# Routing without its weights first: the head of a routed expert stage reordered on three engines

## The chip, the cores and the metric

The kernel runs on one core of one Trainium2 chip. The metric is the device time of one execution in microseconds (us), the median of several runs. The engines are called as in the profile: PE is TensorE, DVE VectorE, ACT ScalarE, POOL GpSimd, and SP SyncE, from which most transfers are issued.

## What is computed

Two transformer blocks run one after the other on 512 tokens of width 1024. All matrix products are in float32, each made of three products of a split into an upper and a lower part. The last stage of the second block, the one that the change touches, is a mixture of experts with a two-level router:

```python
p_grp = softmax(t @ w_rg + b_rg)                 # 4 groups
g_val, g_idx = top_k(p_grp, 1)
le = (t @ w_re + b_re).reshape(n, 4, 4)          # 4 experts in each group
p_exp = softmax(take(le, g_idx))
e_val, e_idx = top_k(p_exp, 2)
weight = g_val * e_val / sum(e_val)
act = silu(t @ w_e_gate[e]) * (t @ w_e_up[e])    # for the chosen experts e
out = sum over the chosen e of weight * act @ w_e_down[e]
```

## The kernel before

Each engine has its own instruction stream, written out by hand, and semaphores order them. Weights stream from HBM in blocks of 1 MB through a ring of four slots (`raw`). ACT rounds a block to its upper part `wh`, DVE subtracts to get the lower part `wl` (`lows`, line 1964, two halves a block), PE multiplies, and its progress (`acc_ready`) frees the slot for SP's next load. In the expert stage a load is issued for each half of a block.

The head of the expert stage goes as follows, in the order of the data.

1. PE brings the router's 20 logits per token into `acc`. DVE's `route()` (lines 2656 to 2717) works on tiny tiles, 128 partitions by 4 to 80 numbers. Each instruction waits for the one before it (`link`). It scales and biases the logits, takes a softmax over the groups (ACT makes the exponential), finds the first maximum (`best`), selects that group's four expert logits, takes a softmax again, finds the two best, and writes `chosen` (a 0/1 mask of token by expert) and `tokx` (token numbers). Then it splits the lower half of the stage's third block (`lows(B0["moe"] + 2)`) and works out the weights (`wtwo`, `gateg`).
2. In the meantime PE transposes the normalised tokens (line 1204), ACT copies them out (`HN`, line 1826, after each of the two exponentials, line 1820) and SP stores them to HBM as `XD`.
3. PE counts with `chosen` (line 1212) which slot each token gets. DVE turns the counts into `posn`, sets the flag `crowded`, and compares positions with a count to make one-hot matrices `G1` (line 2724, four of them, one for each expert of the first group; line 2735 for a whole group). PE multiplies them with the token numbers (`slot_rows`, line 1091), DVE writes the row numbers `rows_in`, and POOL gathers the rows of `XD` into `XSL` by indirect DMA (line 454).
4. PE transposes the gathered rows (`turn_slots`, line 1105), ACT and DVE make `XH` and `XL` of them (`slots_upper` line 1748, `slots_lower` line 2764; the semaphores `f_xh` and `f_xl`), and `gathered(0, first=True)` begins: eight blocks of gate and up products, `b` = 0 to 7, two per expert, then four blocks of down products. Its body is the `Else` arm of a branch on `crowded` that every engine takes; the inputs here take that arm.

In the first group PE goes on so: block 0, the transpositions of the third expert's rows (0, 2), block 1, those of (0, 3), block 2, then rows of the next group. A transposition waits until `f_xl` says that the XL parts of the expert before are written, since it reuses their PSUM banks. On DVE the order is: product of block 0's activation (line 2777), `lows` of block 3, `slots_lower(0, 2)`, and so on. `give_rows_first` writes the row numbers for the results. They are not used before the first scatter. `keep_busy` (line 486) issues products whose results nobody reads; each appears as two rows of a matmul.

Of the kernel before, what the change touches and what calls it, by code (L numbers as in the profile page):

```python
# [12 lines left out]
P = 128  # L13
# [89 lines left out]
def build(nc, xT, memT, wstream, params, consts, lora, poolw, normf, out):  # L103
    with ExitStack() as ctx:
# [233 lines left out]
        def bank(hh, x):  # L338

            return (mb if hh else acc)[:, x if hh else 2 + x, :]  # L340

        def rows_bank(g, e=1):
# [132 lines left out]
        def _(pe):  # L475
# [622 lines left out]
            def turn_slots(i, e):  # L1098

                pe.wait_ge(s[f"in_row{e}"], i * 16 + 16)  # L1100
                pair = 0 if isinstance(i, int) and (i, e) == (0, 1) else 2
                if not isinstance(i, int) or (i, e) > (0, 1):
                    pe.wait_ge(s["f_xl"], i * 8 + 2 * e)
                for k in range(KT):
                    last = nc.tensor.transpose(acc[:, pair + k // 4, (k % 4) * P:(k % 4 + 1) * P],
                                               XSL[:, e, k * P:(k + 1) * P], ident)
                last.then_inc(s["f_tx"], 1)
# [9 lines left out]
            def gathered(i, first=False, last_group=False):  # L1117

                n0, t0 = B0["moe"], T0["moe"]
                if first:  # L1120
                    pe.wait_ge(s["f_toke"], 8)
                    keep_busy(mb[:, 3, :], 6)

                    pe.wait_ge(s["f_xl"], 4)

# [93 lines left out]
            crowded = pe.value_load(flag[0:1, 0:1])  # L1219
            slot_rows(1)  # L1220
            turn_slots(0, 0)
            turn_slots(0, 1)
            with pe.If(crowded > 0):
                pe.wait_ge(s["f_mask"], 2)
                norm_spread(7)
                with pe.Fori(0, 3) as i:
                    group("moe", i, 8, need=(xn_ready, 33), spread=spread_gate)
                group("moe", 3, 8, spread=spread_gate)
                pe.wait_ge(x_ready, 32 + KT)
                for q in range(8):  # L1230
                    if q >= 2:
                        pe.wait_ge(s["xf_ready"], q - 1)
                    turn_rows(q)
            with pe.Else():
                gathered(0, first=True)
                with pe.Fori(1, 3) as i:
                    gathered(i)
                gathered(3, last_group=True)
# [3 lines left out]
        def _(act):  # L1242
# [500 lines left out]
            def slots_upper(i, e):  # L1743

                act.wait_ge(s["f_tx"], i * 4 + (e + 1))
                pair = 0 if isinstance(i, int) and (i, e) == (0, 1) else 2
                for h in range(2):
                    actv(XH[:, 4 * h:4 * h + 4, e * P:(e + 1) * P], acc[:, pair + h, :].rearrange("p (k c) -> p k c", k=4),
                         ACT.Copy).then_inc(s["f_xh"], 1)
# [117 lines left out]
        def _(dve):  # L1867
# [788 lines left out]
            def route():  # L2656
# [6 lines left out]

                def best(p, eq, top, hot):

                    link(v.tensor_reduce(red(top), r(p), AX.X, ALU.max))
                    link(v.tensor_tensor(r(eq), r(p), wide(top), ALU.is_equal))
                    link(v.tensor_tensor(r(eq), r(eq), rank, ALU.mult))
                    link(v.tensor_reduce(red(23), r(eq), AX.X, ALU.max))
                    link(v.tensor_tensor(r(hot), r(eq), wide(23), ALU.is_equal))  # L2670

                def softmax_in(src, to):
                    link(v.tensor_reduce(red(0), src, AX.X, ALU.max))
                    v.tensor_tensor(r(to), src, wide(0), ALU.subtract).then_inc(s["rt_sub"], 1)

                def softmax_out(p):
                    link(v.tensor_reduce(red(0), r(p), AX.X, ALU.add))
                    link(v.reciprocal(red(22), red(0)))
                    link(v.tensor_tensor(r(p), r(p), wide(22), ALU.mult))

# [32 lines left out]
                link(v.tensor_tensor(r(6), r(6), wide(20), ALU.mult))  # L2713
                link(v.tensor_tensor(wtwo[:, 0, :], red(14), red(20), ALU.mult))
                link(v.tensor_tensor(wtwo[:, 1, :], red(17), red(20), ALU.mult))
                for g in range(4):
                    link(v.tensor_tensor(gateg[:, g], r(6), r(5)[:, :, g:g + 1].to_broadcast([P, TT, 4]), ALU.mult))

# [40 lines left out]
            def slots_lower(i, e):  # L2759
                pair = 0 if isinstance(i, int) and (i, e) == (0, 1) else 2  # L2760
                for h in range(2):
                    dve.wait_ge(s["f_xh"], i * 8 + (2 * e + h + 1))
                    dst = slice(4 * h, 4 * h + 4), slice(e * P, (e + 1) * P)
                    v.tensor_tensor(XL[:, dst[0], dst[1]], acc[:, pair + h, :].rearrange("p (k c) -> p k c", k=4),
                                    XH[:, dst[0], dst[1]].bitcast(F32), ALU.subtract).then_inc(s["f_xl"], 1)
# [250 lines left out]
```

## Time and profile before

| | us |
|---|---|
| median of 3 runs | 1656.53 |
| lowest and highest | 1651.3 and 1659.92 |
| the profiled execution | 1651.62 |
| its span, first to last instruction | 1649.7 |
| PE busy in the span | 1528.5 (93%) |
| DVE busy | 1095.7 (66%) |
| ACT busy | 705.2 (43%) |

The profiled execution is 1.92 us longer than its span, which is what lies around it. The stretch that the change rewrites lasts from 1402 to about 1440 us of that span. Of PE's matmuls the ends are modelled, and two that follow each other overlap in the rows.

### The profile page before, as it was taken

What the parts mean: (1) busy time and instruction counts of PE and PEld (TensorE: products, weight loads), DVE (VectorE), ACT (ScalarE), POOL (GpSimd) and SP (SyncE); (2) the same over time, 40 slices, a digit from 0 to 9 for tenths busy, and PEclk for the clock granted to TensorE, in tenths of its full rate; (3) what the DMA queues carried; (4) which work ended last, traced back from release to release, by engine and by line L of the source; (5) the groups of instructions that cost most, each with busy time, mean ns of one, the idle gap of its engine ahead of it and who ended that gap; (6) DMA issues with size and microseconds to landing.
All of it is one profiled execution on the core that took longest, in us unless ns stands there. A gap on an engine that the chain in (4) does not pass through costs nothing.

```text
span 1649.7 us, 26802 instructions
## 1 busy us (share of the span) xinstructions
PE 1528.5 (93%) x11012; PEld 1283.9 (78%) x11012; DVE 1095.7 (66%) x1661; ACT 705.2 (43%) x1057; POOL 62.4 (4%) x53
## 2 busy tenths in 40 slices
PE   5999988998999999999999999999999889889892
PEld 4889776876878888888878787877799657788892
DVE  5831667686489647737689998354765436677875
ACT  5422334444354333333454232334344345367783
POOL 0000000000000000000000000000000000222221
PEclk9999999999999999999999999999999999999996
DMA  6220000002422222222312222232234202478895
GB/s 250 102 90 13 2 2 3 3 3 78 153 77 79 101 102 102 90 90 102 128 51 103 100 79 102 77 126 92 102 128 154 77 18 85 164 244 309 313 315 188
DMA packets 37831, 181.37 MB, mean 110 GB/s; under 512 B 6342, under 2 KB 6470, under 8 KB 24400
## 3 DMA queue, kind: packets, MB, share of 16 engines
q1 hardware_dynamic: 30672, 167.08, 28.6%
q0 software_dynamic: 4864, 8.40, 1.5%
q10 hardware_dynamic: 2176, 4.19, 0.7%
q8 instruction: 87, 1.43, 0.4%
q14 instruction: 32, 0.26, 0.0%
HBM read 175.46 MB, written 12.58 MB: 114 GB/s over the span
## 4 chain that ended last, share of the span: by engine, by line
PE 71%; DVE 18%; ACT 4%; DMA 4%; issue 3%; POOL 0%; DVEq 0%; POOLq 0%; SPq 0%; ACTq 0%
PE acc L480 18%; PE acc L482 18%; PE acc L481 18%; DMA raw<-wstream 3%; DVE CA L2445 2%; PE acc L731 2%; PE mb L731 1%; DVE wl L1976 1%; DVE wl L1964 1%; PE acc L1038 1%; PE mb L562 1%; ACT wh L1273 1%; ACT wh L1260 1%; PE mb L480 1%; PE mb L481 1%
## 5 line engine op out<-in xcount | busy, mean ns | idle before, releaser
L480 PE MATMUL acc<-XH,wh 128*128 128x512 f32 x1008 | 396.2, 393 | 2.3 <-DVE wl L1976 1.3
L482 PE MATMUL acc<-XH,wl 128*128 128x512 f32 x1008 | 392.3, 389 | 0.0
L481 PE MATMUL acc<-XL,wh 128*128 128x512 f32 x1008 | 392.2, 389 | 0.0
L1273 ACT ACTIVATE wh<-raw 128x2048 fp32r<-128x2048 f32 x99 | 189.4, 1915 | 241.6 <-DMA raw<-wstream 241.6
L1976 DVE TENSOR_TENSOR wl<-raw,wh 128x2048 fp32r<-128x2048 f32 x99 | 226.1, 2287 | 67.2 <-ACT wh L1273 64.0
L480 PEld LDWEIGHTS acc<-XH,wh 128*128 128x128 f32 x1008 | 189.3, 188 | 44.6 <-issue 3.3
L481 PEld LDWEIGHTS acc<-XL,wh 128*128 128x128 f32 x1008 | 189.3, 188 | 40.6 <-issue 1.9
L482 PEld LDWEIGHTS acc<-XH,wl 128*128 128x128 f32 x1008 | 189.2, 188 | 39.6
L1294 ACT ACTIVATE ev<-acc 128x512 f32<-128x512 f32 x146 | 85.6, 598 | 218.7 <-PE acc L482 189.6
L1964 DVE TENSOR_TENSOR wl<-raw,wh 128x1024 fp32r<-128x1024 f32 x96 | 116.3, 1221 | 31.7 <-ACT wh L1260 23.7
L1260 ACT ACTIVATE wh<-raw 128x1024 fp32r<-128x1024 f32 x96 | 101.0, 1061 | 20.8 <-DMA raw<-wstream 19.0
L480 PE MATMUL acc<-wh,XH 128*128 128x256 f32 x320 | 94.2, 294 | 3.2 <-DVE tmp L2777 2.6
L482 PE MATMUL acc<-wh,XL 128*128 128x256 f32 x320 | 90.4, 283 | 0.0
L481 PE MATMUL acc<-wl,XH 128*128 128x256 f32 x320 | 90.4, 282 | 0.0
L2445 DVE SCALAR_TENSOR_TENSOR CA<-APAD,par,CA 128x512 f32<-128x512 f32 x120 | 82.1, 746 | 0.5
L480 PE MATMUL acc<-HH,wh 128*128 128x512 f32 x176 | 68.5, 389 | 0.0
L481 PE MATMUL acc<-HL,wh 128*128 128x512 f32 x176 | 68.5, 389 | 0.0
L482 PE MATMUL acc<-HH,wl 128*128 128x512 f32 x176 | 68.5, 389 | 0.0
L480 PEld LDWEIGHTS acc<-wh,XH 128*128 128x128 f32 x320 | 61.1, 191 | 4.0 <-DVE wl L1964 1.8
L481 PEld LDWEIGHTS acc<-wl,XH 128*128 128x128 f32 x320 | 61.2, 191 | 0.0
L482 PEld LDWEIGHTS acc<-wh,XL 128*128 128x128 f32 x320 | 61.1, 191 | 0.0
L444 POOL MEMSET XSL<- 128x4096 f32 x1 | 3.5, 3512 | 1397.6 <-PE mb L482 1397.6
(534 smaller groups left out, 2796.8 us busy)
## 6 DMA issues: line engine op xcount, KB each, us to landing
raw<-wstream SPq DMA_DIRECT2D x99, 1024.0 KB
raw<-wstream SPq DMA_DIRECT2D x96, 512.0 KB
YG<-YT ACTq DMA_DIRECT2D x8, 512.0 KB
XT<-xT SPq DMA_DIRECT2D x2, 1024.0 KB, 9.6
XT<-xT SPq DMA_DIRECT2D x1, 2048.0 KB, 7.7
XD<-HN SPq DMA_DIRECT2D x4, 512.0 KB, 2.6
out<-XTK SPq DMA_DIRECT2D x4, 512.0 KB, 2.6
cst<-consts SPq DMA_DIRECT2D x1, 1230.0 KB, 18.4
```

Of the source, the lines that this page charges most:

```text
L480: mm(out_, a[0], b[0], start=start, stop=False)
L481: mm(out_, a[0], b[1], start=False, stop=False)
L482: return mm(out_, a[1], b[0], start=False, stop=stop)
L562: mm(mb[:, 0, :], ones, sq[:, k % 2, :], start=(k == 0), stop=(k == KT - 1)).then_inc(sq_used, 1)
L731: last = mm(out_[hp(c), t * HD:(t + 1) * HD], left(hp(c), t), right(hp(c), t), start=True, stop=True)
L1038: last = mm(acc[:, v, :], VX[:, j, h * 256 + v * P:h * 256 + (v + 1) * P], PTx[:, j, :], start=(j == 0), stop=(j == 1))
L1260: actv(wh[:, slot, 4 * h:4 * h + 4].rearrange("p a b c -> p (a b c)"), raw[:, slot, h * BLK // 2:(h + 1) * BLK // 2], ACT.Copy).then_inc(h ...
L1273: actv(wh[:, n % RING].rearrange("p a b c -> p (a b c)"), raw[:, n % RING, :], ACT.Copy).then_inc(hi_done, 1)
L1294: actv(ev[:, ring, 2:S + 2], acc[:, bank, :], func, scale=scale).then_inc(evac, 1)
L1964: v.tensor_tensor(wl[:, slot, 4 * h:4 * h + 4].rearrange("p a b c -> p (a b c)"), raw[:, slot, c], wh[:, slot, 4 * h:4 * h + 4].rearrange( ...
L1976: v.tensor_tensor(wl[:, slot].rearrange("p a b c -> p (a b c)"), raw[:, slot, :], wh[:, slot].rearrange("p a b c -> p (a b c)").bitcast(F3 ...
L2445: ins = v.scalar_tensor_tensor(out=CA[:, c, :], in0=x, scalar=w, in1=CA[:, c, :], op0=ALU.mult, op1=ALU.add)
```

## The change

`route()` finds the maxima on the logits less their maximum instead of on probabilities, so that only comparisons stand ahead of `chosen`. The two exponentials are still made by ACT, but read only by the new `route_weights()`. The work that follows `chosen` is put elsewhere: `lows(B0["moe"] + 2)`, `give_rows_first()` and `route_weights()` come after `slots_lower(0, 1)`. PE branches on `crowded` right after its 12 `keep_busy` products, ahead of `slot_rows(1)` and the first transpositions. The rows of the second expert are transposed into banks of `mb` in place of `acc` (`slot_bank`), so the first matmul needs one XL half (`f_xl` 1) instead of four. The `keep_busy` ahead of it shrinks from 6 to 2.

```diff
+        def slot_bank(i, e, h):
+            return mb[:, 2 + h, :] if isinstance(i, int) and (i, e) == (0, 1) else acc[:, 2 + h, :]
...
                 if first:
-                    pe.wait_ge(s["f_toke"], 8)
-                    keep_busy(mb[:, 3, :], 6)
-
-                    pe.wait_ge(s["f_xl"], 4)
+                    keep_busy(acc[:, 0, :], 2)
...
             crowded = pe.value_load(flag[0:1, 0:1])
-            slot_rows(1)
-            turn_slots(0, 0)
-            turn_slots(0, 1)
+            def first_slots():
+                slot_rows(1)
+                pe.wait_ge(s["f_toke"], 8)
+                turn_slots(0, 0)
+                turn_slots(0, 1)
+
             with pe.If(crowded > 0):
+                first_slots()
...
             with pe.Else():
+                first_slots()
                 gathered(0, first=True)
...
-                def softmax_in(src, to):
+                def first_of(eq, hot):
                     link(v.tensor_reduce(red(23), r(eq), AX.X, ALU.max))
                     link(v.tensor_tensor(r(hot), r(eq), wide(23), ALU.is_equal))
...
+                def under_top(src, to, hot):
                     link(v.tensor_reduce(red(0), src, AX.X, ALU.max))
                     v.tensor_tensor(r(to), src, wide(0), ALU.subtract).then_inc(s["rt_sub"], 1)
-                def softmax_out(p):
-                    link(v.tensor_reduce(red(0), r(p), AX.X, ALU.add))
-                    link(v.reciprocal(red(22), red(0)))
-                    link(v.tensor_tensor(r(p), r(p), wide(22), ALU.mult))
+                    dve.wait_ge(s["rt_sub"], 1 if to == 1 else 2)
+                    link(v.scalar_tensor_tensor(out=r(3), in0=r(to), scalar=0.0, in1=rank, op0=ALU.is_equal, op1=ALU.mult))
+                    first_of(3, hot)
...
-                softmax_in(lg[:, :, 0:4], 1)
-                dve.wait_ge(s["rt_exp"], 2)
-                softmax_out(2)
-                best(2, 3, 4, 5)
-                for t in range(TT):
-                    link(v.tensor_tensor(rt3[:, t], lg[:, t, 4:20].rearrange("p (g e) -> p g e", g=4),
-                                         rt[:, 5, 4 * t:4 * t + 4].unsqueeze(2).to_broadcast([P, 4, 4]), ALU.mult))
+                under_top(lg[:, :, 0:4], 1, 5)
+                link(v.tensor_tensor(rt3[:, :, :, :], lg[:, :, 4:20].rearrange("p t (g e) -> p t g e", g=4),
+                                     r(5).unsqueeze(3).to_broadcast([P, TT, 4, 4]), ALU.mult))
                 link(v.tensor_reduce(r(10), rt3[:, :, :, :].rearrange("p t g e -> p t e g"), AX.X, ALU.add))
-                softmax_in(r(10), 11)
-                dve.wait_ge(s["rt_exp"], 3)
-                softmax_out(12)
-                best(12, 13, 14, 15)
+                under_top(r(10), 11, 15)
-                link(v.scalar_tensor_tensor(out=r(16), in0=r(15), scalar=-2.0, in1=r(12), op0=ALU.mult, op1=ALU.add))
-                best(16, 13, 17, 18)
-                link(v.tensor_tensor(red(19), red(14), red(17), ALU.add))
-                link(v.reciprocal(red(20), red(19)))
-                link(v.tensor_tensor(red(20), red(20), red(4), ALU.mult))
+                link(v.scalar_tensor_tensor(out=r(16), in0=r(15), scalar=-1e30, in1=r(11), op0=ALU.mult, op1=ALU.add))
+                link(v.tensor_reduce(red(17), r(16), AX.X, ALU.max))
+                link(v.tensor_tensor(r(13), r(16), wide(17), ALU.is_equal))
+                link(v.tensor_tensor(r(13), r(13), rank, ALU.mult))
+                first_of(13, 18)
...
-                lows(B0["moe"] + 2)
+            def route_weights():
+                dve.wait_ge(s["rt_exp"], 3)
...
             crowded = dve.value_load(flag[0:1, 0:1])
-            give_rows_first()
             place(1)
             place_rows(1)
             slots_lower(0, 0)
             slots_lower(0, 1)
+            lows(B0["moe"] + 2)
+            give_rows_first()
+            route_weights()
             dve.wait_ge(in_rest, 64)
             with dve.If(crowded > 0):
```

On PE, from the load of the flag (`TENSOR_LOAD`) to the stage's first product in the taken arm (`L480 ... <-wh,XH`), before. The rows between the branch and that arm belong to the other arm:

```order
L1219 TENSOR_LOAD flag [waits f_flag]
L1091 MATMUL mb<-tokx,G_143 128x2 [waits f_g]
L1091 MATMUL mb<-tokx,G_143 128x2 x15
L1105 MATMUL acc<-cst,XSL 128x128 [waits in_row0]
L1105 MATMUL acc<-cst,XSL 128x128 x7
L1105 MATMUL acc<-cst,XSL 128x128 [waits in_row1]
L1105 MATMUL acc<-cst,XSL 128x128 x7
L1223 COMPARE_AND_BRANCH
...
L486 MATMUL mb<-cst 128x128 [waits f_toke]
L486 MATMUL mb<-cst 128x128 x5
L480 MATMUL acc<-wh,XH 128x256 [waits f_xl,split_done]
```

and in the changed kernel, the same stretch:

```order
L1219 TENSOR_LOAD flag [waits f_flag]
L1228 COMPARE_AND_BRANCH
...
L1095 MATMUL mb<-tokx,G_143 128x2 [waits f_g]
L1095 MATMUL mb<-tokx,G_143 128x2 x15
L1108 MATMUL acc<-cst,XSL 128x128 [waits in_row0,f_toke]
L1108 MATMUL acc<-cst,XSL 128x128 x7
L1108 MATMUL mb<-cst,XSL 128x128 [waits in_row1]
L1108 MATMUL mb<-cst,XSL 128x128 x7
L490 MATMUL acc<-cst 128x128 x2
L484 MATMUL acc<-wh,XH 128x256 [waits f_xl,split_done]
```

The branch moved from behind the two sets of eight transpositions to ahead of the 16 slot products, the second set goes to `mb`, and the dummy products fell from six to two.

On DVE, before, from the load of the flag to the branch; `place_of` and the first `rows_out` belong to `give_rows_first`, `G_143` is `G1`:

```order
L2839 TENSOR_LOAD flag [waits f_flag]
L2756 COPY place_of<-mb 128x2
L2756 COPY place_of<-mb 128x2 [waits dchain]
L2742 SCALAR_TENSOR_TENSOR place_of<-place_of,cst 128x4 [waits dchain]
L2744 TENSOR_TENSOR rows_out<-place_of 128x4 [waits dchain]
L2734 COPY pcur<-posn 128x16 [waits dchain]
L2735 TENSOR_TENSOR G_143<-cst,pcur 128x2048 [waits dchain]
L2750 TENSOR_SCALAR rows_in<-mb 128x4 [waits f_count]
L2742 SCALAR_TENSOR_TENSOR place_of<-mb,cst 128x4
L2744 TENSOR_TENSOR rows_out<-place_of,mb 128x4 [waits dchain]
L2764 TENSOR_TENSOR XL<-acc,XH 128x4x128 [waits f_xh] x4
L2846 COMPARE_AND_BRANCH [waits in_rest]
```

and in the changed kernel, from the end of `place_rows(1)` on, the rows up to the middle of `route_weights`:

```order
L2772 TENSOR_TENSOR XL<-acc,XH 128x4x128 [waits f_xh] x2
L2772 TENSOR_TENSOR XL<-mb,XH 128x4x128 [waits f_xh] x2
L1970 TENSOR_TENSOR wl<-raw,wh 128x1024 [waits hi_done] x2
L2765 COPY place_of<-mb 128x2
L2765 COPY place_of<-mb 128x2 [waits dchain]
L2751 SCALAR_TENSOR_TENSOR place_of<-place_of,cst 128x4 [waits dchain]
L2753 TENSOR_TENSOR rows_out<-place_of 128x4 [waits dchain]
L2711 TENSOR_REDUCE rt<-rt 128x4 [waits rt_exp,dchain]
L2712 RECIPROCAL rt<-rt 128x4 [waits dchain]
L2713 TENSOR_REDUCE rt<-rt 128x4 [waits dchain]
L2714 TENSOR_TENSOR rt<-rt 128x16 [waits dchain]
L2715 TENSOR_REDUCE rt<-rt 128x4 [waits dchain]
```

Ahead of the branch DVE now has two `wl` halves, the four small instructions of `give_rows_first` and the 13 of `route_weights`; ahead of `G` (here `L2744`) it has four fewer than before.

## Rows read from the trace of the kernel before

**Rows 1.** The page of the profile, part 4: shares of the span in the chain, by engine.

```profile
PE 71%; DVE 18%; ACT 4%; DMA 4%; issue 3%; POOL 0%; DVEq 0%; POOLq 0%; SPq 0%; ACTq 0%
```

**Rows 2.** Stretches of the last stage: us, busy us (instructions) of each engine, PEclk, DMA share, GB/s.

```profile
1474.83:1478.25 3.42, 1.20 (x11) 1.20 (x11) 3.42 (x3) 2.23 (x3) 2.81 (x3) 1.00 0.71 242
1478.25:1485.07 6.82, 6.82 (x33) 6.82 (x33) 2.16 (x2) 1.70 (x3) 2.83 (x2) 0.50 0.71 259
1485.07:1590.00 104.93, 96.12 (x794) 94.23 (x793) 81.08 (x108) 78.58 (x125) 28.47 (x24) 1.00 0.89 314
```

**Rows 3.** The timeline of DVE (VectorE), 1402 to 1415 us: start us, us, what, [idle before].

```profile
1402.43 0.24 DVE L2683 TENSOR_TENSOR lg<-acc,sml 128x80 f32<-128x80 f32 x1
...
1405.31 0.80 DVE L2691 TENSOR_TENSOR rt<-lg,rt 128x16 f32<-128x16 f32 x4
...
1410.83 0.22 DVE L2704 TENSOR_TENSOR chosen<-rt 128x64 fp32r<-128x64 f32 x1
...
1411.18 2.36 DVE L1964 TENSOR_TENSOR wl<-raw,wh 128x1024 fp32r<-128x1024 f32 x2
...
1415.10 0.22 DVE L2832 TENSOR_TENSOR posn<-mb,chosen 128x64 f32<-128x64 f32 x1
```

**Rows 4.** The timeline of ACT (ScalarE), 1406 to 1445 us.

```profile
1406.86 0.22 ACT L1820 ACTIVATE rt<-rt 128x16 f32<-128x16 f32 x1 [1.17 <-DVE rt L2674]
...
1430.16 1.28 ACT L1858 ACT_TABLE_LOAD   x1 [1.57 <-issue]
...
1445.17 1.06 ACT L1260 ACTIVATE wh<-raw 128x1024 fp32r<-128x1024 f32 x1 [1.02 <-DMA raw<-wstream]
```

**Rows 5.** The timeline of PE (TensorE), 1409 to 1449 us.

```profile
1409.76 0.61 PE L486 MATMUL mb<-cst 128*128 128x128 f32 x4
1411.11 0.28 PE L1212 MATMUL mb<-chosen,uptor 128*128 128x16 f32 x1 [0.74 <-DVE chosen L2704]
...
1412.70 3.98 PE L486 MATMUL acc<-cst 128*128 128x128 f32 x20
...
1419.31 2.92 PE L486 MATMUL acc<-cst 128*128 128x128 f32 x24
1423.59 1.95 PE L1091 MATMUL mb<-tokx,G 128*128 128x2 f32 x16 [1.35 <-DVE G L2735]
1425.40 1.97 PE L1105 MATMUL acc<-cst,XSL 128*128 128x128 f32 x16
1428.96 1.60 PE L486 MATMUL mb<-cst 128*128 128x128 f32 x12 [1.60 <-issue]
1430.32 0.36 PE L480 MATMUL acc<-wh,XH 128*128 128x256 f32 x1
...
1438.43 1.06 PE L1105 MATMUL acc<-cst,XSL 128*128 128x128 f32 x8 [1.26 <-DVE XL L2764]
...
1448.83 1.06 PE L1105 MATMUL acc<-cst,XSL 128*128 128x128 f32 x8 [2.52 <-DVE XL L2764]
```

**Rows 6.** The timeline of DVE, 1419 to 1434 us.

```profile
1419.48 0.16 DVE L2729 TENSOR_SCALAR rows_in<-mb 128x1 uint32<-128x1 f32 x1 [0.52 <-PE mb L1091]
1420.10 0.35 DVE L2756 COPY place_of<-mb 128x2 f32<-128x2 f32 x2 [0.45 <-issue]
...
1421.24 2.29 DVE L2735 TENSOR_TENSOR G<-cst,pcur 128x2048 fp32r<-128x2048 f32 x1
...
1427.16 2.48 DVE L2764 TENSOR_TENSOR XL<-acc,XH 128x512 fp32r<-128x512 f32 x4 [1.09 <-ACT XH L1748]
1433.78 0.29 DVE L2777 TENSOR_TENSOR tmp<-acc,tmp 128x128 f32<-128x128 f32 x1 [4.14 <-ACT tmp L1777]
```

**Rows 7.** The timeline of POOL (GpSimd), 1420 to 1425 us.

```profile
1420.15 1.01 POOL L454 DMA_INDIRECT XSL<-XD,rows_in  x1 [0.31 <-issue]
1421.47 2.93 POOL L454 DMA_INDIRECT XSL<-XD,rows_in  x1 [0.31 <-issue]
```

**Rows 8.** The chain that ended last, near 1437 us: start us, us, what.

```profile
1437.35 7.80 DMA raw<-wstream
```

More of the change, by code:

```diff
@@ L1100, in turn_slots @@
                 pe.wait_ge(s[f"in_row{e}"], i * 16 + 16)
-                pair = 0 if isinstance(i, int) and (i, e) == (0, 1) else 2
                 if not isinstance(i, int) or (i, e) > (0, 1):
@@ L1104, in turn_slots @@
                 for k in range(KT):
-                    last = nc.tensor.transpose(acc[:, pair + k // 4, (k % 4) * P:(k % 4 + 1) * P],
+                    last = nc.tensor.transpose(slot_bank(i, e, k // 4)[:, (k % 4) * P:(k % 4 + 1) * P],
                                                XSL[:, e, k * P:(k + 1) * P], ident)
@@ L1745, in slots_upper @@
                 act.wait_ge(s["f_tx"], i * 4 + (e + 1))
-                pair = 0 if isinstance(i, int) and (i, e) == (0, 1) else 2
                 for h in range(2):
-                    actv(XH[:, 4 * h:4 * h + 4, e * P:(e + 1) * P], acc[:, pair + h, :].rearrange("p (k c) -> p k c", k=4),
+                    actv(XH[:, 4 * h:4 * h + 4, e * P:(e + 1) * P], slot_bank(i, e, h).rearrange("p (k c) -> p k c", k=4),
                          ACT.Copy).then_inc(s["f_xh"], 1)
@@ L2662, in route @@
                 rank = cs("rank").unsqueeze(1).to_broadcast([P, TT, 4])
[L2664 to L2668, printed above, removed]
+                def first_of(eq, hot):
                     link(v.tensor_reduce(red(23), r(eq), AX.X, ALU.max))
                     link(v.tensor_tensor(r(hot), r(eq), wide(23), ALU.is_equal))
-                def softmax_in(src, to):
+                def under_top(src, to, hot):
                     link(v.tensor_reduce(red(0), src, AX.X, ALU.max))
                     v.tensor_tensor(r(to), src, wide(0), ALU.subtract).then_inc(s["rt_sub"], 1)
-                def softmax_out(p):
-                    link(v.tensor_reduce(red(0), r(p), AX.X, ALU.add))
-                    link(v.reciprocal(red(22), red(0)))
-                    link(v.tensor_tensor(r(p), r(p), wide(22), ALU.mult))
+                    dve.wait_ge(s["rt_sub"], 1 if to == 1 else 2)
+                    link(v.scalar_tensor_tensor(out=r(3), in0=r(to), scalar=0.0, in1=rank, op0=ALU.is_equal, op1=ALU.mult))
+                    first_of(3, hot)
                 dve.wait_ge(s["rt_lg"], 2)
@@ L2709, in route @@
                                             .to_broadcast([P, TT, 4]), op0=ALU.mult, op1=ALU.add))
-                lows(B0["moe"] + 2)
+            def route_weights():
+                r = lambda j: rt[:, j, :].rearrange("p (t c) -> p t c", t=TT)
+                red = lambda j: rt[:, j, 0:TT]
+                dve.wait_ge(s["rt_exp"], 3)
+                link(v.tensor_reduce(red(0), r(2), AX.X, ALU.add))
+                link(v.reciprocal(red(4), red(0)))
+                link(v.tensor_reduce(red(14), r(12), AX.X, ALU.max))
+                link(v.tensor_tensor(r(16), r(12), r(18), ALU.mult))
+                link(v.tensor_reduce(red(17), r(16), AX.X, ALU.add))
+                link(v.tensor_tensor(red(19), red(14), red(17), ALU.add))
+                link(v.reciprocal(red(20), red(19)))
+                link(v.tensor_tensor(red(20), red(20), red(4), ALU.mult))
                 dve.wait_ge(s["f_mask"], 1)
                 link(v.tensor_tensor(r(6), r(6), r(12), ALU.mult))
-                link(v.tensor_tensor(r(6), r(6), wide(20), ALU.mult))
+                link(v.tensor_tensor(r(6), r(6), red(20).unsqueeze(2).to_broadcast([P, TT, 4]), ALU.mult))
                 link(v.tensor_tensor(wtwo[:, 0, :], red(14), red(20), ALU.mult))
                 link(v.tensor_tensor(wtwo[:, 1, :], red(17), red(20), ALU.mult))
-                for g in range(4):
-                    link(v.tensor_tensor(gateg[:, g], r(6), r(5)[:, :, g:g + 1].to_broadcast([P, TT, 4]), ALU.mult))
+                link(v.tensor_tensor(gateg[:, :, :, :], r(6).unsqueeze(1).to_broadcast([P, 4, TT, 4]),
+                                     r(5).rearrange("p t g -> p g t").unsqueeze(3).to_broadcast([P, 4, TT, 4]),
+                                     ALU.mult))
             def place_first():
@@ L2759, in slots_lower @@
             def slots_lower(i, e):
-                pair = 0 if isinstance(i, int) and (i, e) == (0, 1) else 2
                 for h in range(2):
@@ L2763, in slots_lower @@
                     dst = slice(4 * h, 4 * h + 4), slice(e * P, (e + 1) * P)
-                    v.tensor_tensor(XL[:, dst[0], dst[1]], acc[:, pair + h, :].rearrange("p (k c) -> p k c", k=4),
+                    v.tensor_tensor(XL[:, dst[0], dst[1]], slot_bank(i, e, h).rearrange("p (k c) -> p k c", k=4),
                                     XH[:, dst[0], dst[1]].bitcast(F32), ALU.subtract).then_inc(s["f_xl"], 1)
```

## The prediction

> **What bounds the kernel now.** I read the page's chain first. TensorE (PE) holds 71% of it and VectorE (DVE) 18% [rows 1], so over the whole span PE's own work sets the time, and no change of DVE's small instructions can move more than the places where PE waits for them. The change rewrites one such place, the 40 us in which the router's answer is turned into the first expert's rows. So I read the timelines of the engines there, one by one, and then the stretches behind it.
>
> In the timelines the reader is to look at the bracket, the idle time just before an instruction. PE waits 0.74 us for `chosen`, 1.35 us for the second group's `G1`, 1.60 us for nothing but its own branch, 1.26 us for XL at 1438.43 and 2.52 us for XL at 1448.83 [rows 5]. Between them stand dummy products: 20 rows in 3.98 us, which is 0.20 us each, and 24 in 2.92 us, which is 0.12 each [rows 5]; the first ran mostly at half clock. DVE for its part has one long gap: 4.14 us before the activation product at 1433.78 [rows 6]. Past 1485 us PE is busy 96.12 of 104.93 us [rows 2], so a shift of PE that is still there at 1485 goes through to the end nearly one to one.
>
> **The change, part by part.** Times are those of the profiled execution, in us.
>
> *Router.* From the first `lg` at 1402.43 to `chosen` at 1410.83 [rows 3] there are 38 instructions, 37 steps, in 8.40, so 0.227 a step. In the changed kernel I count 22, so 21 steps: 4.8. `chosen` comes 3.6 earlier. PE can't use all of it. It is in the token transpositions until 1409.76 + 0.61 = 1410.37 [rows 5], and these wait for ACT's copies, three of which stand in front of the second exponential, for which ACT idles 1.17 [rows 4]. That idle time goes, so PE is free at about 1409.2. Counting begins there in place of 1411.11: 1.9 earlier.
>
> *`posn`.* Counting lasts 1412.70 - 1411.11 = 1.6, to 1410.8. Before, DVE was then still in `lows` (2.36, from 1411.18) and the weights, and `posn` ran at 1415.10 [rows 3]. Now nothing stands between: about 1411.0, 4.1 earlier, and the first `G1` is there by about 1412.5. But PE still has its 20 dummy rows to go through. At 3.98 they end at 1414.8, at full clock (20 x 0.12 = 2.4) at 1413.2. I keep 3.98, since PE's work ahead of them is nearly the same. So the slot products, and all that is paced by them, are 1.9 earlier (bounds 1.9 and 3.4), and of 4.1 only that is used.
>
> *Second `G1`.* The last row number moves from 1419.48 to 1417.6. DVE then loads the flag (0.45 of issue) and no longer runs `give_rows_first`: from 1420.10 to 1421.24 stood its four instructions (0.8) and `pcur` [rows 6]. `G1` (2.29) now starts at about 1418.4 and ends at 1420.7; before it ended at 1423.53: 2.8 earlier.
>
> *PE's branch.* After the last slot product PE runs 24 dummy rows (2.92) to 1420.4, where before they ended at 1422.23 and PE waited 1.35 for `G1` [rows 5]. Now it loads the flag (0.45, as on DVE) and takes the branch (1.60) first: 1422.4, which is 1.7 after `G1` is ready. So the moved branch becomes the new wait, and slot products begin 1.2 earlier only (1423.59 before). They and the 16 transpositions last 1427.37 - 1423.59 = 3.8 [rows 5]: 1426.2.
>
> *Gathers.* POOL's issue of a gather takes 1.01, but the one that fell on DVE's 2.29 us `G1` took 2.93 and ended at 1424.40, 0.87 after it [rows 6, 7]. With `G1` at 1418.4 it is the second gather (1420.15 before, 1418.3 now) that is hit: its issue ends at about 1421.6, not 1419.3. Before, its rows were there when PE came to them at about 1426.4, at most 5.2 after the issue's end at 1421.16. Now they come at 1426.8 at the latest, and PE wants them at 1425.3: a wait of 0 to 1.5, of which I take 0.5. This is the lock that the Trainium skill (SBUF — State Buffer, Who interferes with whom) describes: the loser of the port pair that DVE and GpSimd share is blocked outright, not slowed. By that rule the second gather does wait; the trace agrees, 2.93 against 1.01.
>
> *First matmul.* The first XH and XL follow the transpositions: the first XL at 1427.16 [rows 6] moves to 1426.0, and one half (0.62 of the 2.48) is now enough, then two dummies. First matmul at about 1427.0 for 1430.32 [rows 5]: 3.3 earlier. Blocks 0 and 1 and the transposition between them last from 1430.32 to 1437.35, when the load that waits for block 1 is issued [rows 8]: 7.0. They now end at 1434.0.
>
> *DVE, the price.* The last XL ends at 1429.64 before [rows 6], now at about 1428.8. Behind it stand `lows` (2.36), `give_rows_first` (0.8) and 13 small instructions of `route_weights` at 0.20 (the four at 1405.31 took 0.80 [rows 3]), 2.6: 1434.6. Then the branch. PE and ACT show 1.60 and 1.57 of issue at theirs [rows 4, 5]; DVE's lay hidden in its gap of 4.14. I take 1.57: 1436.2. Before, DVE started the activation product at 1433.78 and PE's transposition (0, 3) followed 4.65 later, 0.66 of which DVE waited for ACT; now 4.0 do: 1440.2. That is 1.8 *later* than 1438.43. All the cover that DVE had is used up, and PE, done with block 1 at 1434.0, stands still for 6. With a free branch it would be 1438.6, no change. The Trainium skill (Advanced Engine Details and Errata, Control Flow Timing) gives a compare-and-branch about 108 ns; by it DVE would be at 1434.7 and the transposition at 1438.7. The rows on PE and ACT speak for the longer time.
>
> *Behind it.* Before, PE's stall of 2.52 at 1448.83 came from the load issued at 1437.35, which took 7.80 [rows 8] and kept ACT idle for 1.02 [rows 4]. This load goes out with block 1's end, now 3.3 earlier, so that wait is gone and absorbs up to 1.0. Left: 0.8 later (bounds: free branch 1.0 earlier, no absorption and a gather wait of 1.5, 2.8 later).
>
> *The clock.* In the stretch from 1474.83 PE is busy 1.20 of 3.42 and idles 3.4 in a row before 1477.05; in the next 6.82 its clock is 0.50, 1.2 GHz instead of 2.4 [rows 2]. The new standstill of 6 is longer. If the clock falls the same way, half of 3.4 to 6.8, less the part in which PE stands anyway, is lost: 1 to 3. I give it an even chance and take 0.7 for the middle of a small effect.
>
> **Sum.** 0.8 + 0.7 = 1.5 us later: 1651.62 + 1.5 = 1653.1 for the profiled execution. That execution is 4.9 below the median of the runs, 1656.53, so the forecast for the median is 1658.0: no change that can be told. About 0.5%, 8.3 us, is what a measurement of this kernel can tell from no change.
>
> **The rivals.**
> - *The early start goes through* (2 in 10). If DVE's branch is cheap, the weights are quicker than 0.20 each, and the clock holds, the 3.3 us at the first matmul or the 4.1 at `posn` show at the end: 1 to 4 us less, 1652.5 to 1655.5. For it: every wait on PE up to the first matmul shrinks. Against it: DVE's 5.8 us of moved work in a gap of 4.14 that itself shrinks by 3.3.
> - *The clock falls in the new standstill and again later* (2 in 10, 3 in 100 of them beyond 8.3). The place is PE's wait before the transposition (0, 3). Each half-clock stretch like that at 1478.25 costs up to 3.4 us, once more in the second group 6.8; with 0.8: 1660.7 to 1664. It decides past 8.3 us, so it takes three of the long stretches that the trace before does not have. For it: 6 us of idle time against 3.4 that preceded the fall. Against it: the other head waits, 2.52 and less, were followed by full clock.
> - *The change doesn't do what it says* (1 in 20): the slot products don't come earlier since the token transpositions, not `chosen`, hold PE. Then only the DVE price is left, 2 to 4 us later, 1658.5 to 1660.5.
> - *The forecast*, the gain swallowed by DVE's late arrival, -1 to +3: the rest, 55 in 100.
>
> **How the numbers follow.** All cases lie within -4 and +8 of 1656.53 but for the last 3 in 100. The runs before spread from 1651.3 to 1659.92, so the median of a few wanders by 2 or 3 by itself. The range from 1652.0 to 1662.0 leaves out 1 in 10 on either side. Faster by over 0.5% would need 8.3 us, more than twice all that is removed here: 0.02. Slower: 0.04. Within: 0.94.
>
> **What would show it.** In the profile after: `chosen` about 3.6 earlier after the first `lg` than the 8.40 of before; the slot products bound by dummy rows, with no wait for `G1` behind the branch; one long POOL issue, now the second; the first matmul about 3.3 earlier; DVE without any gap between the last XL and the activation product, and PE waiting some 6 us for XL before the second single set of eight transpositions; perhaps half clock there. The prediction is wrong if DVE reaches the activation product before 1434, if PE's standstill is under 3 us, or if a wait that I don't see, on a late gather or load, comes in the second group.

## The result and the profile after

The changed kernel takes 1661.84 us (median of 12 runs, 1657.1 to 1674.57); the kernel before, timed beside it, 1656.82 (12 runs, 1651.3 to 1661.66). The ratio is 1.0043, with a 95% interval from 1.0027 to 1.0059: 4 to 10 us slower. I had forecast no change that can be told, and this one can. (The ratio is not that of the two medians, which are 5.0 us apart; where a ratio is turned into microseconds below, it is multiplied by 1656.) The profiled execution took 1665.13 us with a span of 1663.2.

Single executions start the stage at slightly different times, so I count from the first `lg` (1402.43 before, 1403.09 after). First DVE's timeline after, which answers to [rows 3, 6]:

```profile
1403.09 0.24 DVE L2685 TENSOR_TENSOR lg<-acc,sml 128x80 f32<-128x80 f32 x1
...
1407.73 0.23 DVE L2699 TENSOR_TENSOR chosen<-rt 128x64 fp32r<-128x64 f32 x1
...
1412.58 0.23 DVE L2840 TENSOR_TENSOR posn<-mb,chosen 128x64 f32<-128x64 f32 x1 [4.53 <-PE mb L1212]
...
1418.19 2.29 DVE L2744 TENSOR_TENSOR G<-cst,pcur 128x2048 fp32r<-128x2048 f32 x1
...
1427.15 1.29 DVE L2772 TENSOR_TENSOR XL<-mb,XH 128x512 fp32r<-128x512 f32 x2
1428.35 2.35 DVE L1970 TENSOR_TENSOR wl<-raw,wh 128x1024 fp32r<-128x1024 f32 x2
...
1433.86 0.23 DVE L2724 TENSOR_TENSOR gateg<-rt 128x64 f32<-128x64 f32 x1
1440.34 0.29 DVE L2785 TENSOR_TENSOR tmp<-acc,tmp 128x128 f32<-128x128 f32 x1 [6.26 <-issue]
```

The router is as short as worked out: `chosen` comes 4.64 after `lg` in place of 8.40. DVE then waits 4.53 for the count, since PE is still at the token transpositions. The late work ends at 1434.09, 31.0 after `lg`. Then comes the row to look at: 6.26 us in which DVE waited for no other engine ("issue"), ahead of the first instruction in the taken arm.

PE's timeline after, which answers to [rows 5]:

```profile
1412.32 2.48 PE L490 MATMUL acc<-cst 128*128 128x128 f32 x20
...
1417.13 2.92 PE L490 MATMUL acc<-cst 128*128 128x128 f32 x24
1422.17 1.95 PE L1095 MATMUL mb<-tokx,G 128*128 128x2 f32 x16 [2.12 <-issue]
...
1426.99 0.56 PE L484 MATMUL acc<-wh,XH 128*128 128x256 f32 x1
...
1444.24 1.94 PE L1108 MATMUL acc<-cst,XSL 128*128 128x128 f32 x8 [9.67 <-DVE XL L2772]
```

PE's load of the flag and its own branch are the new wait ahead of the slot products (2.12). The first matmul is 23.90 after `lg` in place of 27.89, so 4.0 were won up to there. The transposition (0, 3) is 41.15 after it in place of 36.00: PE stood 9.67 us ahead of it.

POOL's timeline, which answers to [rows 7]; the issue under `G` is the third, with 2.07, and the second was free:

```profile
1417.97 1.01 POOL L458 DMA_INDIRECT XSL<-XD,rows_in  x1 [0.31 <-issue]
1419.28 2.07 POOL L458 DMA_INDIRECT XSL<-XD,rows_in  x1 [0.30 <-issue]
```

Stretches after, with the columns of [rows 2]:

```profile
1434.00:1438.90 4.90, 0.58 (x5) 0.37 (x4) 0.09 (x1) 2.40 (x4) 0.00 (x0) 1.00 0.78 234
1438.90:1449.10 10.20, 4.86 (x23) 4.89 (x24) 7.51 (x10) 1.09 (x2) 0.99 (x1) 0.50 0.14 46
...
1483.30:1493.50 10.20, 9.55 (x44) 9.55 (x45) 4.09 (x4) 2.16 (x4) 4.38 (x3) 0.50 0.58 206
```

and the second of these stretches of the kernel before:

```profile
1438.90:1449.10 10.20, 7.68 (x67) 7.51 (x66) 7.68 (x12) 7.00 (x13) 1.36 (x1) 1.00 0.82 273
```

The standstill has two followers. The clock falls to 0.50 (1.2 GHz) within it, at 1438.90, for 10.2 us, of which PE works only from 1444.24 on; and it stands there again for 10.2 at 1483.3, where before it was 6.82. And the weight stream stops: the DMA moves 46 GB/s in place of 273. SP's next load waits 13.6 us for PE's progress, since no block is used up and no slot of the ring comes free.

### The profile page after: what moved, and what is told of

The parts are those of the page before. It is cut to its first block, busy times and chain, and to the rows that moved or that the text cites. A ratio compares the mean times of both kernels' runs of the same rounds, so it can differ in the third digit from the quotient of the medians.

```text
span 1663.2 us, 26778 instructions
## 1 busy us (share of the span) xinstructions
PE 1537.1 (92%) x11004; PEld 1291.6 (78%) x11004; DVE 1093.7 (66%) x1650; ACT 705.5 (42%) x1057; POOL 61.5 (4%) x53
## 3 DMA queue, kind: packets, MB, share of 16 engines
q8 instruction: 86, 1.41, 0.4%
## 4 chain that ended last, share of the span: by engine, by line
PE 70%; DVE 18%; ACT 4%; DMA 4%; issue 3%; POOL 0%; DVEq 0%; POOLq 0%; SPq 0%; ACTq 0%
PE acc L484 18%; PE acc L486 18%; PE acc L485 18%; DMA raw<-wstream 3%; DVE CA L2451 2%; PE acc L735 2%; DVE wl L1970 2%; PE mb L735 1%; DVE wl L1982 1%; PE acc L1042 1%; ACT wh L1267 1%; PE mb L566 1%; PE mb L484 1%; PE mb L620 1%; ACT wh L1280 1%
```

## The experiments

Each kernel is compared with the kernel before, timed beside it on the same chip. Unless it is said otherwise, a ratio is over 10 to 12 runs of the kernel.

**1. What the parts are worth.** The first five undo or do one part.

`e1_dve_back`, the changed kernel with

```diff
             route()
+            lows(B0["moe"] + 2)
+            route_weights()
...
-            lows(B0["moe"] + 2)
             give_rows_first()
-            route_weights()
```

> The changed kernel with one part undone: DVE splits the third block's lower half and works out the weights directly behind `chosen`, where it waits 4.53 us for the count in the profile after, in place of ahead of its branch. Theory A (the moved work puts DVE's branch at 1434, where fetching the branch's target takes 6.3 us among the weight loads, and PE stands 9.7 us): DVE branches at about 1429, reaches the activation product by 1433, PE's stall before the transposition (0, 3) falls under 3 us, and the time is 1652 to 1655, 2 to 5 us below the kernel before. Rival R (the loss comes from PE: fewer dummy products and a clock that falls, or from the branch moved on PE): the time stays at about 1660 to 1663 and half-clock stretches remain at 1425 and 1439.

Measured: 1.0016 (1.0004 to 1.0029).

`e2_branch_first`, the changed kernel with DVE's branch directly behind the last XL, and the moved work in both arms.

> The changed kernel, with DVE's branch taken directly behind the last XL and the three moved pieces of work behind it, in both arms; the same instructions in another place. Theory A1 (the branch is long because its code fetch competes with the weight loads that run from 1430 on): branch of 1.5 to 3 us at 1428.4, activation product at about 1437, the transposition (0, 3) at about 1440 to 1441 in place of 1444.2, time about 1657 to 1659. Rival A2 (DVE's branch into this arm always costs 6.3 us, wherever it stands): transposition at 1444 as in the changed kernel, time about 1662.

Measured: 1.0021 (1.0003 to 1.0038).

`e3_pe_side`, the kernel before with PE's part alone: the branch ahead of the slot products, `slot_bank`, two dummies, the first matmul behind one XL half.

> The kernel before, with only the PE side of the change: branch ahead of the slot products, second rows into other banks, one XL half before the first matmul, two dummies for six. DVE's order and arithmetic are those of before. Theory A: the first matmul about 1.5 us earlier than 1430.32, DVE still in time, so 1 to 2 us below the kernel before, hardly to be told. Rival R (PE's side is what costs): 2 to 5 us above it.

Measured: 1.0020 (1.0004 to 1.0036).

`e4_moved_only`, the kernel before with `lows`, `give_rows_first` and the weights (old arithmetic) behind the last XL.

> The kernel before, with only DVE's work moved: the lower half of the third block, the weights and `give_rows_first` go ahead of DVE's branch, in the old arithmetic. Theory A: DVE reaches the branch at about 1432 to 1434, waits for its code among the loads, and PE's transposition (0, 3) comes 3 to 6 us later than 1438.43; time 2 to 6 us above the kernel before. Rival R: the earlier `posn` (about 2 us) wins and the time is that of before or 2 us less.

Measured: 0.9989 (0.9976 to 1.0003).

`e5_route_only`, the kernel before with the new router arithmetic, and `lows` and `route_weights` directly behind `chosen`.

> The kernel before, with only the new arithmetic: comparisons on logits, then the lower half of the third block and the weights directly behind `chosen` and ahead of `posn`; everything else as before. Theory A: `posn` about 2.5 us earlier, the slot products 1.9 earlier, no work moved ahead of DVE's branch, so about 2 us below the kernel before. Rival R: no part of the change saves anything, time as before.

Measured: 0.9967 (0.9945 to 0.9989).

So the router alone wins 5.5 us (0.33% of 1656; the interval reaches from 1.8 to 9.1). DVE's late work costs nothing on the slow router (`e4`), and something on the fast one (`e1` is 0.27% better than the changed kernel). PE's part costs by itself (`e3`). Theory A was right on `e5` alone: it wanted `e1` below the kernel before, `e4` above it and `e3` no slower. In `e2` DVE's branch took 2.76, as A1 had it, and the transposition (0, 3) came 2.0 earlier after the first `lg` than in the changed kernel.

**2. What DVE's branch takes, and when.** `e6_loads_held` is the changed kernel with `sp.wait_ge(s["f_hid"], 1)` ahead of `load_range(103, 147)`, so that the weight loads start after block 0. `e7_marker` is the kernel before with a one-element memset first in DVE's taken arm; it makes visible when DVE gets there. `e8_arm_shifted` is the changed kernel with 96 memsets in the arm that is not taken, which moves the taken arm's addresses.

> The changed kernel, with SP's weight loads of the expert stage's fifth block and on held back until DVE has made its first activation product, behind its branch. The branch then stands at the same place in time, 1434.1, but no weight load runs. Theory A1 (code fetch competes with loads): the idle time before the activation product falls from 6.26 to 1.5 to 2.5 us. Rival A2 (fixed cost or distance of the code): it stays 6 us or more. The whole is slower or equal, since loads start 5 us later.

> The kernel before with one tiny DVE instruction at the very start of the taken arm, so that the end of the branch is seen, which lay hidden in a gap of 4.14 us. Theory A1: it starts 1.5 to 3 us after the last XL. Rival A2: about 6 us, which would make the activation product late here too.

> The changed kernel with 96 more instructions in DVE's other arm, which is not taken, so that the target of the branch lies elsewhere in the code. Theory A1: the idle time before the activation product stays near 6.3 us, 5 to 7. Rival A3 (where the target falls in a page of code decides): it changes by 2 us or more.

Measured: `e6` 1.0029 (1.0004 to 1.0055); `e7` and `e8` were run once each, so they have profiles and no ratio. DVE's timelines, the first instruction behind the branch in `e7`, `e4`, `e6`, `e8` and `e1`, in this order, one fence for each:

```profile
1434.89 0.06 DVE L2870 MEMSET most<- 128x1 f32 x1 [3.25 <-issue]
```
```profile
1436.67 0.29 DVE L2782 TENSOR_TENSOR tmp<-acc,tmp 128x128 f32<-128x128 f32 x1 [3.24 <-issue]
```
```profile
1441.98 0.29 DVE L2786 TENSOR_TENSOR tmp<-acc,tmp 128x128 f32<-128x128 f32 x1 [3.49 <-issue]
```
```profile
1437.24 0.29 DVE L2785 TENSOR_TENSOR tmp<-acc,tmp 128x128 f32<-128x128 f32 x1 [5.16 <-issue]
```
```profile
1436.34 0.29 DVE L2785 TENSOR_TENSOR tmp<-acc,tmp 128x128 f32<-128x128 f32 x1 [4.68 <-issue]
```

The branch takes 3.2 us even in its old place, twice what I took. `e6` (3.49) lies between its two theories. `e8` (5.16) stayed in the range of A1, and the change by 2 us that A3 wanted did not come. The DMA view shows what moves in the meantime. Of the changed kernel, from the end of the last weight to 1438.4 and from there to DVE's restart:

```profile
q8 instruction: 1, 0.02, 1.3%
```
```profile
DMA packets 149, 0.48 MB, mean 247 GB/s; under 512 B 33, under 2 KB 33, under 8 KB 148
...
q14 instruction: 1, 0.01, 1.6%
```

One instruction packet of queue q14 comes in the second stretch and none in the first; I take it for code of the taken arm. Its start in the packet records, beside the last instruction's end and the restart (us):

| kernel | end | q14 packet | restart | end to packet | packet to restart |
|---|---|---|---|---|---|
| `e4` | 1433.43 | 1434.84 | 1436.67 | 1.41 | 1.83 |
| `e6` | 1438.48 | 1440.15 | 1441.98 | 1.67 | 1.83 |
| `e1` | 1431.65 | 1434.47 | 1436.34 | 2.82 | 1.87 |
| `e8` | 1432.09 | 1435.41 | 1437.24 | 3.32 | 1.83 |
| after | 1434.09 | 1438.50 | 1440.34 | 4.41 | 1.84 |
| `e2` | 1430.84 | 1431.74 | 1433.60 | 0.90 | 1.86 |
| `e13` | 1430.81 | 1433.43 | 1435.26 | 2.62 | 1.83 |
| `e9` | 1436.81 | 1441.30 | 1443.14 | 4.49 | 1.84 |

`e9` and `e13` are from parts 3 and 4 below; in `e9` DVE's instructions are those of the changed kernel. The second part is the same everywhere, 1.83 to 1.87. The first lies between 0.9 and 4.5. The first weight load of the stage was issued 1.0 us before the branch in `e4` (at 1432.39), 4.5 in the changed kernel (1429.60) and 5.1 in `e8` (1427.04), and in `e6` it was held until after block 0. In `e2` it went out 0.7 after the branch began, in `e13` 2.5 before it and in `e9` 4.6. So in most of the kernels the packet comes late where loads have long been under way. `e1` does not fit (load at 1432.04, 0.4 after), nor does `e8` beside the changed kernel, and `e6` changes the loads' whole schedule. That the code stands in line behind the loads is thus likely and not shown. Shifting the arm's addresses (`e8`) left a long wait.

The Trainium skill (Runtime: NRT & Kernel Launch, Instruction fetch mechanics) says that a taken branch to a page that isn't loaded forces a transfer of that page before execution goes on. By that rule the packet stands between branch and restart; the trace agrees, with one packet 1.84 us ahead of the restart.

**3. Is it the clock?** `e9_stall_filled` is the changed kernel with 30 dummy products in the standstill, `e12_route_filled` is `e5` with dummies in its smaller waits.

```diff
+                    if first and b == 1:
+                        keep_busy(mb[:, 3, :], 30)
```

> The changed kernel, with 30 dummy products on PE between block 1 and the wait for the transposition (0, 3), about 7 us of the 9.7 us in which it stood still. DVE's late arrival stays as it is. Theory C (the main cost is the clock: it falls after PE has stood or done narrow work, and falls back to 1.2 GHz in the stretch from 1439 to 1449): that stretch stays at full clock, the time spent at half clock drops by 6 us or more on the mean, and the time by 2 to 4 us, to about 1658. Theory D (the late DVE itself shifts all that follows): no change, 1660 to 1663.

> A version that the runs so far point to: the kernel before with the new arithmetic of the router alone, and dummy products where PE waits in the first group, 5 before the transposition (0, 3), 9 before the one at 1449, 12 before the slot products at 1477. Theory C: the 6.8 us at half clock after 1478 become rare, time at half clock falls by 5 us or more against the router alone, and the time by 2 us, to about 1651, some 5 below before. Theory D: the dummies delay or do nothing, time as with the router alone, about 1653.

Measured: `e9` 1.0042 (1.0025 to 1.0060), `e12` 0.9967 (0.9951 to 0.9984). In `e9` the first `lg` is at 1405.58, 2.5 later than in the changed kernel. Its stretches: the filled wait, the half clock behind it and that of the second group; then, in its own fence, the second group's place in `e12`:

```profile
1434.00:1444.00 10.00, 9.88 (x87) 9.68 (x85) 3.23 (x16) 5.54 (x10) 0.99 (x1) 1.00 0.71 236
1448.10:1451.50 3.40, 3.40 (x19) 3.40 (x18) 2.46 (x4) 1.09 (x2) 1.29 (x1) 0.50 0.07 11
...
1485.70:1492.50 6.80, 6.48 (x30) 6.48 (x31) 2.54 (x3) 0.41 (x2) 4.05 (x3) 0.50 0.58 203
```
```profile
1470.00:1485.00 15.00, 14.28 (x123) 14.09 (x122) 11.57 (x12) 10.43 (x16) 9.47 (x7) 1.00 0.79 261
```

The fill of `e9` left 3.4 us at 0.50 behind the standstill in place of 10.2, and 6.8 in the second group in place of 10.2; that of `e12` kept 1.00 in the second group. Over all runs the time at half clock (worked out as at the end of the next section) fell from 65.1 to 56.5 us, and from 50.1 in `e5` to 44.6 in `e12`. Neither fill moved the time (1.0042 against 1.0043, 0.9967 against 0.9967). So the clock in these stretches is not what the change costs.

**4. Which part on PE.** `e10_pe_six` is `e3` with six dummies, `e11_before_two` the kernel before with two.

> The kernel before with the PE side of the change, but with the six dummy products of before ahead of the first matmul in place of two. Theory C1 (the four dummies taken away let the clock fall at 1425 to 1428): the time is again that of before, the half-clock stretch near 1428 gone. Theory C2 (the branch ahead of the narrow slot products, 2 us of standing and then little work, lets it fall): half clock near 1418 to 1428 and some 3 us above before, as with two dummies.

> The kernel before with two dummy products in place of six ahead of the first matmul, and nothing else. Theory C1: time 1 to 3 us above before, with a half-clock stretch near 1430. Theory C2: time as before or 1 us less.

Measured: 1.0012 (0.9995 to 1.0029) and 1.0003 (0.9988 to 1.0018). The number of dummies makes no difference that these intervals can tell (`e10` against 1.0020 for `e3`). That left the branch and the banks:

```diff
-            def first_slots():
-                slot_rows(1)
-                pe.wait_ge(s["f_toke"], 8)
-                turn_slots(0, 0)
-                turn_slots(0, 1)
+            slot_rows(1)
+            pe.wait_ge(s["f_toke"], 8)
+            turn_slots(0, 0)
+            turn_slots(0, 1)
             with pe.If(crowded > 0):
-                first_slots()
```

is `e13_branch_back` on the changed kernel, `e14_both_back` on `e1` and `e16_banks_only` on `e3`. `e15_branch_only` moves nothing but the branch in the kernel before.

> The changed kernel with TensorE's branch back at its old place, behind the 16 transpositions of the first slots; the new banks, the first matmul that waits for half an XL and the whole of VectorE's late work stay. Theory P (it is the early branch of TensorE that costs): about half of the loss goes, ratio 1.0015 to 1.0025, with the branch's 1.6 us behind the transpositions and not ahead of the slot products. Theory D (what costs is that VectorE comes late to the product behind block 1, with its branch of 6.3 us): nothing is won, ratio 1.003 to 1.005, since VectorE's work between the last XL and the activation product is the same, and TensorE, if anything earlier, waits 9 to 11 us ahead of its second set of eight transpositions.

> The kernel with VectorE's work directly behind `chosen` (dve_back, 1.0016) and TensorE's branch back too; the new banks, two dummy rows and the late `give_rows_first` are what is left of the change beside the router. Theory P: 0.996 to 0.998, as with the router alone (0.9967). Theory Q (banks, two dummy rows and a first matmul on half an XL cost): about 1.001 as in dve_back. If it is under 0.9967 beyond the interval, it is the best version.

> The kernel before with one edit: slot products and transpositions are written in both arms behind TensorE's branch, everything else is old. Theory P: 1.001 to 1.003, the whole of what the PE side alone cost (1.0020), with the second row of slot products 1 to 2 us later than before. Theory Q: 1.000.

> The kernel before with the new banks, two dummy rows and the first matmul behind half an XL, and TensorE's branch at its old place. Theory P: 0.998 to 1.000, the first matmul about 1 us earlier. Theory Q: 1.001 to 1.003.

Measured: `e13` 1.0006 (0.9993 to 1.0020), `e14` 0.9967 (0.9951 to 0.9983), `e15` 1.0018 (1.0001 to 1.0034), `e16` 0.9993 (0.9978 to 1.0008). Theory P holds on `e14`, `e15` and `e16`, and `e13` won more than the half that it allowed; Q falls with `e14` and `e16`. Theory D, that DVE's lateness is all, falls with `e13`, though D's own part is there: `e13` is 0.39% above `e14`.

Four of these make a square, all with the new router and banks. Ratio, and in brackets the start of the transposition (0, 3) after the first `lg`:

| | DVE's work behind `chosen` | behind the last XL |
|---|---|---|
| PE's branch behind the transpositions | `e14` 0.9967 (32.67) | `e13` 1.0006 (36.87) |
| ahead of the slot products | `e1` 1.0016 (34.94) | after 1.0043 (41.15) |

PE's timeline, the waits for the second slot products and for (0, 3), in `e14`, `e13` and `e1`:

```profile
1421.05 1.95 PE L1095 MATMUL mb<-tokx,G 128*128 128x2 f32 x16 [0.49 <-DVE G L2738]
...
1436.11 1.06 PE L1108 MATMUL acc<-cst,XSL 128*128 128x128 f32 x8 [1.25 <-DVE XL L2766]
```
```profile
1419.11 1.95 PE L1095 MATMUL mb<-tokx,G 128*128 128x2 f32 x16 [0.48 <-DVE G L2738]
...
1439.16 1.94 PE L1108 MATMUL acc<-cst,XSL 128*128 128x128 f32 x8 [5.01 <-DVE XL L2766]
```
```profile
1424.61 1.95 PE L1095 MATMUL mb<-tokx,G 128*128 128x2 f32 x16 [2.28 <-issue]
...
1440.24 1.07 PE L1108 MATMUL acc<-cst,XSL 128*128 128x128 f32 x8 [3.21 <-DVE XL L2772]
```

Behind the transpositions PE's branch is not free either: in `e14` it takes 2.70, and PE restarts at 1427.53, when the first XL half has been there for 2.2 us.

```profile
1424.62 1.29 DVE L2766 TENSOR_TENSOR XL<-acc,XH 128x512 fp32r<-128x512 f32 x2 [1.09 <-ACT XH L1748]
```
```profile
1427.53 0.71 PE L490 MATMUL acc<-cst 128*128 128x128 f32 x4 [2.70 <-issue]
1427.99 0.36 PE L484 MATMUL acc<-wh,XH 128*128 128x256 f32 x1
```

But there it delays PE alone, while the gathered rows, XH and XL are made beside it. The early branch gives the first matmul almost nothing: it comes 24.25 after `lg` in `e1` for 24.55 in `e14`, and 23.90 in the changed kernel for 23.51 in `e13`. And ahead of the slot products (2.28 in `e1`) all that hangs on the rows is about 2 later: the last XL ends 25.70 after `lg` for 23.66, DVE's branch comes behind it, and (0, 3) is 2.27 later. DVE's late work adds 4.20 alone and 6.2 on top of the early branch. From `e13` to the changed kernel (0, 3) moves by 4.28: the late work ends 2.48 later (31.0 after `lg` for 28.52), and DVE's branch takes 6.26 for 4.46.

## Why the prediction was wrong

- *Router.* Right. 4.64 for 4.8. `e5` and `e14` show 5.5 us of gain by it; with 1.8 and 2.8 us at the low ends of their intervals, that can't be told from the 3.3 that I let reach the first matmul.
- *Count and `posn`.* `posn` came 9.49 after `lg`; I had it at about 8.6. Right in kind: PE's transpositions and dummies pace it. Counting began 7.67 after `lg` for my 6.8, since some of the transpositions ran at half clock (eight in 1.94 us at 1404.99, where eight took 1.21 before). The 20 dummies took 2.48, my other bound, so I had kept the wrong end (3.98).
- *PE's branch.* Right in itself: 2.12 us idle for 2.05 (0.45 and 1.60), and slot products 1.69 after the end of `G` for 1.7. But I booked it only as a gain forgone. `e13` prices it at 0.37% (6.1 us); it moves DVE's late work by 2.5 as well.
- *Gathers.* Wrong object, no effect: the third issue was hit and not the second. The rule that I cited from the Trainium skill (SBUF — State Buffer, Who interferes with whom) holds by half here. An issue that begins inside `G` is held past its end, 2.07 against 1.01. But the second issue began at 1417.97, ahead of `G` (1418.19), so by the rule `G` should have waited, and it took its 2.29.
- *First matmul.* 4.0 earlier for 3.3.
- *DVE, the price.* This is the step that failed: "PE and ACT show 1.60 and 1.57 of issue at theirs; DVE's lay hidden in its gap of 4.14. I take 1.57". It measured 6.26. A third of the miss (1.6 of 4.7) is that DVE's branch isn't PE's or ACT's: in the old place it takes 3.2 (`e7`), within the bound of 4.14, of which I took the low end. The other 3 us came with the new place, where the old gap bounds nothing; what makes it long there stays open (part 2 above). With 6.26 PE's standstill became 9.67 where I had 6, and (0, 3) came 5.2 late, not 1.8. The late work before the branch was well sized, its end 31.0 after `lg` for 32.2. My bound for a free branch was off too: 0.2 later less 1.0 is 0.8 earlier, not 1.0. The Trainium skill's figure of about 108 ns for a compare-and-branch (Advanced Engine Details and Errata, Control Flow Timing) is further off still; the trace has 1.50 us on ACT, 2.12 on PE (with the load of the flag) and 6.26 on DVE.
- *Behind it.* "This load goes out 3.3 earlier and absorbs up to 1.0" came and did not help. PE's wait of 2.52, two sets behind (0, 3), was 1.35:

```profile
1450.36 1.04 PE L1108 MATMUL acc<-cst,XSL 128*128 128x128 f32 x8
1455.72 1.06 PE L1108 MATMUL acc<-cst,XSL 128*128 128x128 f32 x8 [1.35 <-DVE XL L2772]
```

  But from (0, 3) to the set before that wait it took 6.12 for 3.88 (1442.31 before). The loads stopped during the standstill, and the third `G` of the timeline (1481.60 for 1474.70) was 6.2 late after `lg`.
- *The clock.* The pattern of that rival came, 10.2 and 10.2 us at 0.50, and its range (1660.7 to 1664) holds the median. Its cause did not: `e9` took most of the first stretch away and won nothing. The right end of the range came from the wrong reason.
- *What can be told.* I had allowed 0.5%, 8.3 us; the interval of the result is 0.16% to either side, 2.7 us.
- *The early start goes through* was denied by (0, 3), and *the change doesn't do what it says* by the first matmul.

The sum, as the ratios have it: router -5.5 us (`e14`), DVE's late work +6.5 (`e13` less `e14`), PE's early branch on top of it +6.1, together +7.1, by the way they are taken. From the medians beside the kernel before, the same steps are -4.3, +6.5 and +2.8, together +5.0, so the size of the last one is uncertain. I had a gain wholly swallowed and a remainder of 0.8 + 0.7.

Open is why the losses are larger in the total than at (0, 3): PE's branch is 2.3 us at the head with DVE's work early, and 0.49% (8.1 us) in the ratio. `e1` even has (0, 3) 1.06 earlier than the kernel before, and is slower. Its profiled execution, 1653.08, was the fastest of its 12, so the trace can't show where the loss lies. From the clocks and spans of its 12 runs, `e1` averages 60.7 us at half clock (mean of (1 - clock) x 2 x span), `e14` 48.4, the changed kernel 65.1 and the kernel before 53 to 55; so something behind the head differs, that the two fills did not touch. Half clock can cost at most half of its length, here 6.2 of the 8.1 us between `e1` and `e14`; among the changed kernel's 12 runs each us more of it goes with 0.41 us more time. So the clock elsewhere may be part of it, or the later groups, or the weight stream, and no run here separates them. `e4` says the same from the other side: (0, 3) 1.9 late on the old router, and no loss.

No version beats `e5` and `e14`, 0.9967: the new router, with PE's branch and DVE's work where they were.

## What to carry to other kernels

A taken branch can cost an engine several microseconds (2.8 to 6.3 on DVE here), and its price is that engine's own, at that place: bound it by a marker first in the taken arm before moving it, and don't take it from another engine. Leave it behind the work that others wait for; in front of that work, its full length is passed on. A gain at the head of a chain is kept only if what was put behind the head doesn't end later than the work that it once hid under.

## What the hardware showed

- From the start of q14's instruction packet to DVE's restart it is 1.83 to 1.87 us in eight kernels; the time from the last instruction's end to that packet varies between 0.90 and 4.49.
- The same branch on DVE takes 2.76 us (`e2`), 3.2 in its old place, and 6.26 and 6.32 in the changed kernel and `e9`, with the loads more than 4 us under way.
- Keeping PE busy through a wait shortened the half clock behind it from 10.2 to 3.4 us, and the kernel was no faster.
- A wait of one engine stops the weight stream too: 46 GB/s for 10.2 us, where it was 273.
